# Other start addresses for TensorE's stationary weights in a two-layer hybrid decoder trunk

## The reference, cut to what matters

```python
for l in range(DEPTH):                                   # DEPTH = 2
    h = rms_norm(x, attn_norm[l])
    proj = h @ w_in[l]                                   # 1024 x 3104, the in-projection
    ...                                                  # three groups of heads read parts of proj
    x = x + mix @ w_out[l]                               # 1024 x 1024
    h2 = rms_norm(x, ffn_norm[l])
    gate, up = jnp.split(h2 @ w_gate_up[l], 2, axis=-1)  # 1024 x 5632
    x = x + (jax.nn.silu(gate) * up) @ w_down[l]         # 2816 x 1024
```

## Time and profile before

| what | value |
|---|---|
| median of 3 timed runs | 1330.0 us (1329.96 to 1330.1) |
| the profiled execution's own time | 1329.44 us |
| its span, first to last instruction | 1327.7 us |
| TensorE matmul records | 8936, busy 1318.8 us (99% of the span) |
| TensorE weight loads | 8936, busy 1160.9 us (87%) |
| VectorE, ScalarE, GpSimd busy | 740.3, 625.9, 649.8 us |
| DMA queue q1 | 30.2% of 16 engines' span |

### The profile page before, as it was taken

How to read it: one execution, slowest core, us unless ns; L and a number is a source line. 1 busy time by engine, 2 the same in 40 slices (tenths; PEclk the granted TensorE clock), 3 DMA queues, 4 the chain that set the end, 5 groups by cost and what they waited for, 6 DMA issues and landing times.

```text
span 1327.7 us, 22375 instructions
## 1 busy us (share of the span) xinstructions
PE 1318.8 (99%) x8936; PEld 1160.9 (87%) x8936; DVE 740.3 (56%) x1450; ACT 625.9 (47%) x1223; POOL 649.8 (49%) x454
## 2 busy tenths in 40 slices
PE   8999999999999999999999999999999999999999
PEld 7888887778899889998879888887888998899987
DVE  6637777722876137771165387777248751477611
ACT  5563436636556225652335543467356642256511
POOL 4458307644454544554343663177435554354552
PEclk9999999999999999999999999999999999999999
DMA  7316300115334224333222352001233333334322
GB/s 174 123 38 161 96 17 1 34 43 93 95 96 118 97 88 114 110 96 119 88 86 78 75 165 71 1 2 33 64 96 88 104 96 111 96 96 122 102 89 86
DMA packets 176583, 114.91 MB, mean 87 GB/s; under 512 B 48224, under 2 KB 154976, under 8 KB 176480
## 3 DMA queue, kind: packets, MB, share of 16 engines
q1 hardware_dynamic: 174368, 113.22, 30.2%
q10 hardware_dynamic: 2112, 0.26, 0.1%
HBM read 109.80 MB, written 3.67 MB: 85 GB/s over the span
## 4 chain that ended last, share of the span: by engine, by line
PE 94%; DVE 2%; POOL 1%; ACT 1%; issue 1%; DMA 0%; SPq 0%; DVEq 0%
PE ps L807 35%; PE ps L1288 28%; PE ps L857 7%; PE ps L1189 7%; PE ps L946 2%; PE ps L1094 2%; PE ps L1133 2%; PE ps L1116 2%; PE ps L1103 1%; PE ps L872 1%; PE ps L1142 1%; POOL arena L1924 1%; PE ps L926 1%; PE ps L1055 1%; PE ps L748 1%
## 5 line engine op out<-in xcount | busy, mean ns | idle before, releaser
L1827 POOL TENSOR_TENSOR w_lo<-w_raw,w_hi 128x2048 fp32r<-128x2048 f32 (+2 forms) x59 | 264.2, 4479 | 313.0 <-ACT w_hi L1393 245.4
L1393 ACT ACTIVATE w_hi<-w_raw 128x2048 fp32r<-128x2048 f32 (+2 forms) x61 | 113.9, 1867 | 232.0 <-PE ps L807 161.4
L1845 POOL TENSOR_TENSOR aT_lo<-ffn_tmp,aT_hi 128x512 fp32r<-128x512 f32 x44 | 63.4, 1440 | 164.5 <-ACT aT_hi L1440 164.5
L2573 DVE SCALAR_TENSOR_TENSOR x_tok<-ps,st,x_tok 128x512 f32<-128x512 f32 x32 | 23.8, 750 | 144.3 <-PE ps L807 144.3
L807 PE MATMUL ps<-w_hi,aT_hi 128*128 128x512 f32 x352 | 95.8, 390 | 0.0
L807 PE MATMUL ps<-w_lo,aT_hi 128*128 128x512 f32 x352 | 95.5, 389 | 0.0
L807 PE MATMUL ps<-w_hi,aT_lo 128*128 128x512 f32 x352 | 95.4, 389 | 0.0
L1401 ACT ACTIVATE w_hi<-w_raw 128x512 fp32r<-128x512 f32 x38 | 24.2, 636 | 129.7 <-PE ps L1288 93.8
L807 PE MATMUL ps<-hT_hi,w_lo 128*128 128x512 f32 x320 | 81.0, 393 | 0.0
L807 PEld LDWEIGHTS ps<-w_lo,aT_hi 128*128 128x128 f32 x352 | 66.1, 188 | 13.8
L807 PEld LDWEIGHTS ps<-w_hi,aT_lo 128*128 128x128 f32 x352 | 66.1, 188 | 13.8
(11 more groups left out here) (383 smaller groups left out, 3330.8 us busy)
## 6 DMA issues: line engine op xcount, KB each, us to landing
w_raw<-in_w_gate_up SPq DMA_DIRECT2D x88, 512.0 KB, 5.0
w_raw<-in_w_in SPq DMA_DIRECT2D x21, 1024.0 KB, 5.3
w_raw<-in_w_down SPq DMA_DIRECT2D x16, 1024.0 KB, 5.0
w_raw<-in_w_down SPq DMA_DIRECT2D x8, 768.0 KB, 4.4
w_raw<-in_w_out SPq DMA_DIRECT2D x16, 256.0 KB, 4.0
w_raw<-in_w_out SPq DMA_DIRECT2D x8, 512.0 KB, 4.9
w_raw<-in_w_in SPq DMA_DIRECT2D x2, 1056.0 KB, 7.3
x_tok<-in_x SPq DMA_DIRECT2D x4, 512.0 KB, 5.0
```

Of the source, the lines that this page charges most:

```text
L1393: nc.scalar.activation(words(whi, c, kt * w), words(raw, c, kt * w), ACT.Copy).then_inc(S["w_hi"], 1)
L1827: nc.gpsimd.tensor_tensor(words(wlo, c, kt * w), words(raw, c, kt * w), words(whi, c, kt * w).bitcast(F32), ALU.subtract).then_inc(S["w_lo ...
L1845: nc.gpsimd.tensor_tensor(alo[:, cnt % FT, :], ft[:, cnt % 2, :], ahi[:, cnt % FT, :].bitcast(F32), ALU.subtract).then_inc(S["a_lo"], 1)
```

## The change

The constant SKEW for the fast blocks stays. Six of the in-projection's "C" chunks and the three plain blocks get an offset of their own, in words: 16, 2, 48, 80, 112 and 18 for chunks 1, 2, 6, 7, 10 and 11, and 16, 2 and 48 for the plain blocks 0, 1 and 2. It is the same in both layers. Chunk 0, the chunks whose weights move, the out-projection and the down projection stay at 0. Instructions, their order, their waits and the transfers are the same; only addresses inside w_hi and w_lo differ.

```diff
@@ -32,6 +32,8 @@
 N_SLOTS = 24
 SKEW = 8
+IN_OFFSETS = {1: 16, 2: 2, 6: 48, 7: 80, 10: 112, 11: 18}
+PLAIN_OFFSETS = (16, 2, 48)
 CMP_SLOTS = (8, 9)
@@ -141,7 +143,11 @@
     def split_offset(c):
 
         cnt = block_of(c)
-        return SKEW if cnt is not None and is_fast(cnt) else 0
+        if c < FFN0:
+            return IN_OFFSETS.get(c, 0)
+        if cnt is not None and not is_fast(cnt):
+            return PLAIN_OFFSETS[cnt]
+        return SKEW if cnt is not None else 0
```

## The result

The changed kernel takes 1333.05 us (median of 11, 1332.66 to 1333.70) against 1329.96 us for the kernel before (median of 11, 1329.80 to 1330.22). The ratio is 1.0023, with a 95% interval of 1.0016 to 1.0031. It is slower by 3.1 us, where 1329.5 was forecast, and the measured time lies just above the range's upper end of 1333.0.

The account below looks back on a forecast made before the run. TensorE's distance between matmul starts was taken as the bound. From the profiled 1329.44 us, kind A 0, kind B -0.5, restarts 0 and split 0 gave 1328.9, in medians 1329.5; 8-in-10 range 1324 to 1333.

Parts of the forecast that it names:

- What bounds the kernel: TensorE, 99% busy without waits in the touched stretches; each nanosecond per matmul start distance enters the end time fully.
- the split: ACT's copy and POOL's subtraction writing the weights 8 to 448 bytes later; claimed to cost nothing.
- Kind A: 576 matmuls at multiples of 64 bytes, chunks 1, 6, 7, 10 and plain blocks 0 and 2; claimed change 0.
- mean of 13.3 ns: Start distance of 288-column matmuls beyond their columns' 120.0 ns; taken to be the same as with no shift.
- Kind B: 288 matmuls 8 bytes past such a multiple, chunks 2 and 11 and plain block 1; claimed 0.5 us gain.
- The 1.7 ns: Gain per matmul, fast blocks shifted 32 bytes (118.3 ns) against unshifted attention scores (120.0); applied to 288 matmuls.
- (a): Rival for all touched matmuls: nothing depends on the address, 1330.0 us; chance 0.2.
- (b): Rival: the 13.3 ns are a read collision, parted by odd 64-byte lines; 1323.7 us, 1320.5 with all; chance 0.22.
- (c): Rival: a slow relation holds for whole chunks, 6.7 ns a matmul; 1331.9, 1333.9 or 1335.8 us; chance 0.17.

Follow-up runs that it names:

- kindA: Kernel before with only the whole 64-byte-line offsets: chunks 1, 6, 7, 10 and plain blocks 0 and 2; the rest at 0; 1332.36 us, ratio 1.0017.
- survey1: Kernel before with a different offset in each in-projection chunk, plain block, down-projection chunk and fast block, to map paces; 1339.12 us, one run.
- u16: Kernel before with all six in-projection chunks and three plain blocks offset by 16 words (64 bytes); 1334.84 us, ratio 1.0035.
- shift_all: Kernel before without offsets in the nine units, spacer tile 16 words larger, so both operands move by 64 bytes; 1330.61 us, ratio 1.0004.
- u64: Kernel before with all six in-projection chunks and three plain blocks offset by 64 words (256 bytes); 1330.56 us, ratio 1.0002.
- kick_both: Kernel before with SKEW 16 for the fast blocks, but weights of each feed-forward half's first fast block at 8 words; 1316.11 us, ratio 0.9894.
- kick_first: Kernel before with SKEW 16 for the fast blocks, but weights of only the first half's first fast block at 8 words; 1322.97 us, one run.

## Why the prediction was wrong

**What bounds the kernel** held. TensorE stays busy through the touched stretches, no wait came in, and 3.1 us of matmul pace became 3.1 us of time. The step from ns per matmul to us, 864 matmuls at full weight, was right, and so was leaving the split and the waits at nothing. What was wrong is the change per matmul.

**Kind A at 0** is the step that failed first. It measures 2.3 us more (kindA), of the 3.1 in all. The ground for the 0 was that 288-column products with relations that move by 128 bytes for each k keep the mean of 13.3 ns over their columns. That mean is true for a stream in which four relations alternate. It does not say that each of them alone gives it: 512 columns at 128 bytes run at 232.0, 5.3 above no shift. The spread inside the same stretch, 292 to 302 ns, was the better witness, and the prediction used it for a bound only. Read to the nanosecond, the starts behind the earlier trace rows are 140 ns apart every fourth time and 130 to 132 the three times between, in step with the four relations. That speaks for the address, where the prediction held that it might follow time as much.

**Kind B at -0.5 us** failed in its sign. The 1.7 ns between the earlier trace rows are real: 256-column matmuls go from 120.0 to 118.4 ns with a shift of 8 words (survey1). Carried to 512 columns and to another shift it was worth nothing: 8 bytes cost 4 ns there and 32 bytes cost 6.7. What is left of the loss without kind A, 0.8 us, is kind B's (0.9 by the table of the result), where 0.5 of gain was forecast. The two widths have different maps.

**The rivals.** (a), no dependence, is ruled out by u16. (b), a collision that an odd number of 64-byte lines resolves, is ruled out by the changed kernel itself. (c) is what happened in kind: 230 or more stands in six of the nine units. Its price of 6.7 ns is the measured one at 64 and 320 bytes; at 8 bytes it is 4 and at 192 it is 2.2, so that the loss is 3.1 us and not (c)'s 5.8 for all. That the price fits so well is luck in part: it is the 140 ns less the mean, and the 140 stands 8 to 9 ns above its own neighbours. It was given 0.17 because a repeated relation seemed no likelier to be bad than good. But the kernel before sits at a relation whose pace is undercut by none of the forty relations of the map, so nearly any move had to cost; the forecast had no row for that and looked for a gain in the neighbourhood of zero. The top of the range, 1333, stopped short of (c) with all of kind A, and the time came out 0.05 us above it.

**The Trainium skill**, "TensorE: Matmul & The Clock Gate", in its section "Step-by-step: what each phase is for" has the two reads on independent ports, so that a weight load steals nothing from the running matmul. u16 against shift_all contradicts that as a rule for the time: moving the weights by 64 bytes alone takes 233.3 ns a matmul, moving both operands 226.7. The measurement decides. The 215.8 ns that the prediction took from the formula in its section "Back-to-back issue gap" was reached by no 512-column stream; the lowest is 226.7.

## What to carry to other kernels

Where TensorE is the bound and weights are reloaded for every matmul, compare the steady distance between starts with the columns' own time. The relative address of the two operands can be moved freely, and here it had another best value for 256 columns than for 512. It has to be measured at the width in question, in a stream as the kernel has it. One map made in small pieces is not enough: the same addresses can settle at two paces, so a candidate must be timed in place. In this kernel one block of 84 matmuls with its weights at another relation, ahead of the others, moved a long stream from the slow pace to the fast one; nothing smaller was tried. A mean over varying relations says nothing about a single one.

## What the runs showed of the hardware

Many of the paces lie at whole steps of 6.7 ns, 16 clocks at 2.4 GHz, over the columns' time: 106.7 + 6.7 = 113.3, 120.0 and 133.3 for 256 columns, 213.3 + 13.3 = 226.7 and 213.3 + 20.0 = 233.3 for 512. Others (228.9, 230.7, 118.4, 117.8) are means of short repeating patterns; at 192 bytes the distances are mostly 226, 229 and 232.

The pace depends on the relation of the two operands (u16 against u64 and shift_all) and on what ran before (kick_both against kick_first). That the cause is the two reads meeting in the same part of SBUF is argued and not shown: no run separates it from another cause with the same signs, and the period of 256 bytes that would go with it holds for 512 columns in part only. What decides which pace a stream falls into is open too, beyond that the matmuls ahead of it do. So it is open as well whether the pairs that break the period, such as 240 and 496 bytes, differ by their relation, by their entry, or because one was measured with weights and the other with activations as the stationary operand; it was not tried.
